# A two-layer transformer trunk: the opening stage in another order, with its sums on ScalarE and its first modulation in column groups

## What is computed

```
sh1, sc1, gt1, sh2, sc2, gt2 = silu(cond) @ w_mod + b_mod          # 1024 -> 6 x 1024
h = rms_norm(x, norm1_g) * (1 + sc1) + sh1
q, k, v, u = h @ w_in                                              # 1024 -> 1280
x = x + gt1 * (concat(attention(q, k, v), pool_mixer(u)) @ w_out)
h2 = rms_norm(x, norm2_g) * (1 + sc2) + sh2
x = x + gt2 * conv_ffn(h2)                                         # 1024 -> 2 x 2816 -> 1024
```

## Time and profile before

| | us |
|---|---|
| median of 3 runs | 1548.91 (1543.1 to 1551.49) |
| the profiled execution | 1550.63 |
| its span in the trace | 1548.7 |
| start of the first `w_first` transfer | 8.26 |
| start of the first projection (`linear_pair` of layer 0) | 61.51 |

### The profile page before, as it was taken

One profiled execution on the slowest core, in us unless ns is written; L12 is line 12 of the kernel. 1 busy time (PEld: TensorE's weight loads), 2 busy tenths in 40 slices (PEclk: granted clock), 3 DMA queues, 4 the chain that ended last, 5 costly groups with the idle time before them and its releaser, 6 DMA issues.

```text
span 1548.7 us, 25735 instructions
## 1 busy us (share of the span) xinstructions
PE 1465.7 (95%) x10321; PEld 1431.0 (92%) x10321; DVE 907.4 (59%) x1366; ACT 519.4 (34%) x744; POOL 409.4 (26%) x266
## 2 busy tenths in 40 slices
PE   6997789999999999999999978998999999999996
PEld 5997668989999999999999967898999999999996
DVE  0497895879683738695646577436944323444333
ACT  2424664252232113223223467425223211323221
POOL 1165100214342004243311530020433200333320
PEclk9999899999999999999999989998999999999998
DMA  8252021514343524343431200031422321222311
GB/s 318 86 164 85 29 68 38 170 50 155 122 132 120 152 72 146 109 151 111 138 94 49 72 28 2 15 97 47 157 68 81 94 70 56 81 68 81 94 57 69
DMA packets 191825, 147.02 MB, mean 95 GB/s; under 512 B 4337, under 2 KB 179065, under 8 KB 190713
## 3 DMA queue, kind: packets, MB, share of 16 engines
q1 hardware_dynamic: 191160, 145.51, 30.4%
q10 hardware_dynamic: 576, 0.26, 0.1%
HBM read 142.87 MB, written 2.88 MB: 94 GB/s over the span
## 4 chain that ended last, share of the span: by engine, by line
PE 87%; DVE 6%; ACT 2%; issue 2%; POOL 1%; DMA 1%; SPq 0%; DVEq 0%; ACTq 0%; POOLq 0%
PE pair L1076 69%; PE pair L1093 5%; PE pair L1341 3%; PE pair L1319 2%; PE pair L1159 2%; PE pair L1306 2%; PE pair L1192 2%; DVE mod_acc L805 1%; DVE small L969 1%; POOL tree L480 1%; DVE q_st L906 1%; ACT tree L692 1%; DVE w_lo L782 1%; PE pair L1146 1%; PE pair L1134 0%
## 5 line engine op out<-in xcount | busy, mean ns | idle before, releaser
L1076 PE MATMUL pair<-in_hi,w_hi 128*128 128x320 f32 x1792 | 411.7, 311 | 7.7 <-DVE w_lo L782 7.7
L1076 PE MATMUL pair<-in_hi,w_lo 128*128 128x320 f32 x1792 | 409.3, 310 | 0.0
L1076 PE MATMUL pair<-in_lo,w_hi 128*128 128x320 f32 x1792 | 408.8, 310 | 0.0
L1076 PEld LDWEIGHTS pair<-in_hi,w_hi 128*128 128x128 f32 x1792 | 300.2, 188 | 9.3 <-issue 6.3
L1024 DVE SCALAR_TENSOR_TENSOR conv<-pair,vec,conv 128x127 f32<-128x127 f32 x352 | 168.8, 541 | 236.3 <-ACT conv L720 236.1
L1076 PEld LDWEIGHTS pair<-in_lo,w_hi 128*128 128x128 f32 x1792 | 300.5, 188 | 0.0
L1076 PEld LDWEIGHTS pair<-in_hi,w_lo 128*128 128x128 f32 x1792 | 300.1, 188 | 0.0
L511 POOL TENSOR_TENSOR silu_a<-silu_a,conv 128x640 f32<-128x640 f32 x44 | 110.8, 2519 | 587.0 <-DVE conv L1024 587.0
L782 DVE TENSOR_TENSOR w_lo<-w_raw,w_hi 128x1024 fp32r<-128x1024 f32 (+1 forms) x152 | 203.8, 1342 | 82.9 <-ACT w_hi L532 82.7
L720 ACT ACTIVATE conv<-pair,vec 128x640 f32<-128x640 f32 x88 | 77.7, 885 | 438.1 <-PE pair L1076 427.4
L805 DVE SCALAR_TENSOR_TENSOR mod_acc<-mod_raw,cond,mod_acc 128x1024 f32<-128x1024 f32 x140 | 221.5, 1623 | 0.1
(11 more groups left out here) (146 smaller groups left out, 1600.9 us busy)
## 6 DMA issues: line engine op xcount, KB each, us to landing
w_raw<-in_w_up_dram SPq DMA_DIRECT2D x88, 512.0 KB, 3.9
mod_raw<-in_w_mod_dram SPq DMA_DIRECT2D x80, 512.0 KB, 4.1
w_raw<-in_w_down_dram SPq DMA_DIRECT2D x32, 704.0 KB, 4.7
w_raw<-in_w_in_dram SPq DMA_DIRECT2D x20, 512.0 KB, 4.2
w_first<-in_w_mod_dram SPq DMA_DIRECT2D x8, 1024.0 KB, 14.2
w_raw<-in_w_out_dram SPq DMA_DIRECT2D x16, 512.0 KB, 3.9
out_dram<-yout SPq DMA_DIRECT2D x5, 512.0 KB, 4.0
xin<-in_x_sample_dram SPq DMA_DIRECT2D x1, 2048.0 KB, 17.6
```

Source lines behind the costliest of these rows:

```text
L1076: ins = pe.matmul(dst[:, a:a + HALF_T], w[:, s, k, :], rhs[:, kk, a:a + HALF_T], start=first and r == 0, stop=last and r == 2)
```

## The change

x is loaded ahead of everything large, in five transfers with a semaphore each. The 14 row transfers go to ScalarE's queue, 5 ahead of its first activation and 9 behind its second. ScalarE squares each token block of `xin` as it lies (1024 columns, tokens on partitions), with a row sum as a by-product (`accum_out`), and takes the root of the five sums; GpSimd's adds and `stat(0)` go. The slices of x are copied out of PSUM by ScalarE (even k, bank `pair[2]`) and VectorE (odd k, bank `pair[3]`). After `spread(0)` VectorE makes `xhat` = x * rstd in the space of `xin`. The modulation swaps its operands: the stationary one is `cond_cols` (two conditioning columns and 30 of zeros), the moving one is `w_first`, 512 columns at a time, and its four quarters write to four groups of 32 partitions of one bank. Its result is copied out by ScalarE, transposed by four matmuls, and read by `mod_finish`. `in_hi` then is one ScalarE instruction from `xhat` with gain and shift, and VectorE makes its own copy of the sum (`sq`) and subtracts. The first load of `mod_raw` waits for the squares, whose scratch it is. Later norms are as before but for their semaphore counts.

```diff
+        cond_cols = mod_acc[:, 0, 0:NK * QUAD].rearrange("p (k r) -> p k r", k=NK)
+        first_rows = mod_acc[:, 1, 0:512]
...
+                xhat = xin[:, :, :].rearrange("p b d -> p (b d)").rearrange("p (k t) -> p k t", k=NK)
...
@@ sync
+            for b in range(NT):
+                src = x_prompt[0] if b == 0 else x_sample[0, (b - 1) * P:b * P, :]
+                sp.dma_start(xin[:, b, :], src).then_inc(s_x[b], 16)
+            for k in range(NK):
                 load_first(k)
+                if k >= NK - 2:
+                    load_in(0, k - (NK - 2))
+            for n in range(2, 4):
+                load_in(0, n)
             sp.dma_start(cst[:, P:n_const], consts[:, P:n_const]).then_inc(s_const, 16)
-            for k in range(4, NK):
-                load_first(k)
-            for n in range(4):
-                load_in(0, n)
+            sp.wait_ge(s_xsq, NT)
...
@@ scalar
+            act_e.activation(cond_cols[:, :, 0:2], pair[2][0:P, 0:2 * NK].rearrange("p (c k) -> p k c", c=2),
+                             ACT.Silu).then_inc(s_c32, 1)
...
+            for b in range(NT):
+                act_e.wait_ge(s_x[b], 16)
+                if b >= 2:
+                    act_e.wait_ge(s_xsq, b - 1)
+                act_e.activation(mod_raw[:, b % 2, :], xin[:, b, :],
+                                 ACT.Square, accum_out=rtok[:, b:b + 1]).then_inc(s_xsq, 1)
+            act_e.wait_ge(s_eps, 2)
+            act_e.wait_ge(s_xsq, NT)
+            act_e.activation(rtok[:, :], rtok[:, :], ACT.Sqrt, bias=eps[:, 0:1], scale=1.0 / D).then_inc(s_sd, 1)
+            for k in range(0, NK, 2):
+                act_e.wait_ge(s_xt, k + 1)
+                act_e.activation(x[:, k, :], pair[2][:, 0:T], ACT.Copy).then_inc(s_xe, 1)
...
+            hi(0, 0, NK)
+            act_e.wait_ge(s_mfirst, NK)
+            act_e.activation(first_rows, pair[0][:, 0:512], ACT.Copy).then_inc(s_frow, 1)
+            hi(1, 1, NK)
...
@@ vector
-            for n in range(2):
-                lo(n, n, NK)
+            for k in range(1, NK, 2):
+                dve.wait_ge(s_xt, k + 1)
+                dve.tensor_copy(x[:, k, :], pair[3][:, 0:T]).then_inc(s_xe_dve, 1)
...
+                dve.tensor_tensor(xhat[:, k, :], x[:, k, :], lin[3], ALU.mult).then_inc(s_xhat, 1)
             dve.wait_ge(s_vec, 1)
+            lo(0, 0, NK)
             for C in range(2):
                 mod_finish(C)
+            lo(1, 1, NK)
...
@@ tensor
                 pe.wait_ge(s_first[k], 16)
-                rhs = cond[:, :, k:k + 1].to_broadcast([P, 2, HALF])
-                for j in range(2 * NK):
-                    a = j % NK * P
-                    ins = pe.matmul(pair[j // NK][:, a:a + P].rearrange("p (i r) -> p i r", i=2),
-                                    w_first[:, k % N_FIRST, j * P:(j + 1) * P], rhs,
-                                    start=k == 0 and j % 4 == 0, stop=k == NK - 1, skip_group_check=True)
+                for j in range(4):
+                    ins = pe.matmul(pair[0][j * QUAD:(j + 1) * QUAD, 0:512], cond_cols[:, k, :],
+                                    w_first[:, k % N_FIRST, j * 512:(j + 1) * 512], start=k == 0, stop=k == NK - 1)
                 ins.then_inc(s_mfirst, 1)
...
+            pe.wait_ge(s_frow, 1)
+            for t in range(4):
+                ins = pe.transpose(pair[1][:, t * P:(t + 1) * P], first_rows[:, t * P:(t + 1) * P], ident)
+            ins.then_inc(s_ft, 1)
```

More of the change, by code:

```diff
@@ L23 @@
 HALF = P // 2
+QUAD = 32
 EPS = 1e-6
@@ L214, in v @@
             return vec[:, L, place[0], ds(place[1] + i, n)]
-        s_const, s_rows, s_x = sem("const_loaded"), sem("rows_loaded"), sem("x_loaded")
+        s_const, s_rows, s_x = sem("const_loaded"), sem("rows_loaded"), [sem(f"x_loaded{b}") for b in range(5)]
         s_crow = sem("cond_rows_loaded")
@@ L448, in sq_slot @@
                 return sq[:, m % 2, :]
-            clear_sum(0)
-            for m in range(NK - 1):
-                add_squares(0, m)
+            pool.memset(cond_cols, 0.0).then_inc(s_c32z, 1)
             for L in range(DEPTH):
@@ L578, in _ @@
                 ins.then_inc(s_vec, 1)
[L579 to L588 removed]
+            hi(0, 0, NK)
+            act_e.wait_ge(s_mfirst, NK)
+            act_e.activation(first_rows, pair[0][:, 0:512], ACT.Copy).then_inc(s_frow, 1)
+            hi(1, 1, NK)
+            act_e.wait_ge(s_gain, 1)
+            act_e.wait_ge(s_mod, 2)
+            for k in range(NK):
+                act_e.wait_ge(s_xhat, k + 1)
+                for ci, a, b in SEG:
+                    act_e.activation(in_hi[:, k, a:b], xhat[:, k, a:b], ACT.Identity,
+                                     scale=gain[:, 0, 0, ci, k:k + 1],
+                                     bias=mod[:, 0, 0, ci, k:k + 1]).then_inc(s_hhi, 1)
             for L in range(DEPTH):
[L590 removed]
+                if L > 0:
+                    norm(2 * L, L, 0)
                 hi_third(tile_in(L) + 2, NK, w_third_in)
@@ L814, in mod_finish @@
                 if C < 2:
[L815 removed]
+                    dve.wait_ge(s_ft, 1)
                 else:
@@ L1200, in _ @@
             pe.transpose(pair[2][:, 0:2 * NK], cond_rows[:, :], ident[0:2 * NK, 0:2 * NK]).then_inc(s_vec_t, 1)
+            pe.wait_ge(s_c32, 1)
             pe.wait_ge(s_cond, 1)
+            for k in range(NK):
+                if k >= 2:
+                    if k % 2 == 0:
+                        pe.wait_ge(s_xe, k // 2)
+                    else:
+                        pe.wait_ge(s_xe_dve, k // 2)
+                for b in range(NT):
+                    if k == 0:
+                        pe.wait_ge(s_x[b], 16)
+                    ins = pe.transpose(pair[2 + k % 2][:, b * P:(b + 1) * P], xin[:, b, k * P:(k + 1) * P], ident)
+                ins.then_inc(s_xt, 1)
+            mod_first(0)
             N_ROW_DMAS = 5 + 4 + 3 + DEPTH
@@ L1204, in _ @@
             for L in range(DEPTH):
-                if L > 0:
+                if L == 0:
+                    pe.wait_ge(s_xe, NK // 2)
+                else:
                     pe.wait_ge(s_vec, L)
```

129 lines of the change are left out of this document (68 added, 61 removed).

## The result

| | before | changed |
|---|---|---|
| median of the runs | 1546.19 us (1543.1 to 1551.49, 4 runs) | 1529.02 us (1524.98 to 1530.1, 4 runs) |
| profiled execution, its span | 1550.6, 1548.7 us | 1529.39, 1527.6 us |
| start of `linear_pair` | 61.51 us | 40.74 us |
| its length | 15.57 us | 16.77 us |
| from its end to the end of the span | 1471.6 us | 1470.1 us |

The ratio of the medians is 0.987 with a 95% interval of 0.9844 to 0.9895: faster by 1.1 to 1.6%. The forecast was 1528.0 us in a range of 1522 to 1539. In the profiled executions the span lost 21.1 us: 20.8 at the start of the first projection, less 1.2 that the projection itself grew, and 1.5 in all that follows.

The account below looks back on a forecast made before the run. TensorE was taken to bound the opening, with memory close behind. Terms up to VectorE's last chain put `linear_pair`'s start at 38.9 instead of 61.51 us: 22.6 off 1550.6 gives 1528.0 us, range 1522 to 1539.

Parts of the forecast that it names:

- x transposes end: TensorE's transposes of the x slices in the opening: end between 21.8 (fast) and 25.0 us (slow), taken as 23.3.
- a modulation step: Eight records of 512 columns on TensorE, all four column groups at once: 0.92 us against 3.99 for the old step.
- spreading ends: TensorE's spreading for the norm, after modulation steps 0 and 1 and the rows: 1.60 us long, ending at 28.8.
- slice 7 lands: Load of the last `w_first` slice, behind `w_in` tile 0: lands at 33.0 us, TensorE and memory arriving together.
- `xhat` ends: VectorE's eight `xhat` slices from 28.8 us, 0.82 each, end at 35.4 and lead its chain to the projection's start.
- rival (1): Modulation: only two records run at a time, a step takes 1.84 us, start 45.1, time 1534.2; chance 0.22.
- The plain shift: After the opening: its gain arrives unchanged at the end, 1487 us from projection start to span end, within 3 us.
- half clock: First projection: left at 15.57 us; half clock lasting twice as long would lose 1.9 us, put into the range only.
- (2): Modulation: the four groups run one after another, start 59.9 us, time 1549.0, no change; chance 0.08.
- (3): Modulation: groups run serially and TensorE stays at half clock for half the steps, start 76.5, time 1565.6; chance 0.05.
- (4): ScalarE's row issues cost twice SP's, squares start 6.3 us later, start about 45, time 1534; chance 0.05.
- (5): Stage up to 155 us: a free-running load gives the gain back later, up to all of it, 1550; chance 0.02.

Follow-up runs that it names:

- early_slices: Changed kernel with slice 6 of `w_first` in its own space and slice 7 loaded ahead of `w_in` tile 0; 1528.35 us, ratio 0.9871 to the kernel before.
- kept_busy: Changed kernel with extra matmuls that nothing reads in TensorE's waits around the last modulation step; 1526.31 us, ratio 0.9852 to the kernel before.
- two_groups: Changed kernel with two column groups in each of two banks and two copies by ScalarE; 1527.64 us, ratio 0.986 to the kernel before.
- one_group: Changed kernel with all four modulation quarters on one group of 32 partitions, in four banks, with four copies; 1544.53 us, ratio 0.9972 to the kernel before.
- rows_on_sync: Changed kernel with the parameter rows back on SP's queue, ahead of x; 1533.09 us, ratio 0.9907 to the kernel before.
- the first four experiments: Changed kernel with one column group (1544.53 us), two (1527.64) or the old modulation shape (1542.87); the kernel before with the column groups alone (1542.78).

## Why the prediction was right, and where its terms were off

| step of the sum | said | measured |
|---|---|---|
| root done | 16.2 | 15.5 |
| x transposes end | 23.3 | 21.9 |
| a modulation step | 0.92 | 0.86 |
| spreading ends | 28.8 | 26.5 |
| slice 7 lands | 33.0 | 34.85 |
| last step ends | 34.4 | 36.88 |
| `xhat` ends | 35.4 | 32.5 |
| projection starts | 38.9 | 40.74 |
| its length | 15.57 | 16.77 |
| from its start to the span's end | 1487 | 1486.9 (second execution 1482.9) |

**Right.** Four groups at once, the largest term: the two records of the earlier trace rows that start before either's second record were the evidence, and it carried over from two groups to four. The Trainium skill, "TensorE: Matmul & The Clock Gate", Part 3, gives 3.07x for four row groups; here four column groups do in 0.86 us what one does in 3.43, a factor of 4.0, more than the page has for four. The prediction took the same part's rule, that matmuls start and end strictly in program order, to speak for rival (1), and wrote that the trace does not agree. It read its own rows too coarsely. In stretches of 0.01 us at line 1341 of the kernel before, one record is at work first and two from the next stretch on:

```profile
187.70:187.71 0.01, 0.01 (x1) 0.01 (x2) 1.00 0.00 0
187.71:187.72 0.01, 0.01 (x2) 0.01 (x2) 1.00 0.00 0
```

At line 1257 now it is one in 26.40:26.41, two in 26.41:26.42, four in 26.42:26.43. So the trace agrees with the page's order of starts. What decides the time is that a group doesn't wait for another group's second record, which comes 0.43 us later.

**Right, but with too narrow a test.** The plain shift was right too: the earlier trace rows had no load behind the projection that runs ahead by itself, and over twelve executions with ends from 53.2 to 77.1 us the remainder behind the first projection stayed within 1466.3 to 1473.0. But the prediction called itself wrong if the length from the projection's start to the end of the span differed from 1487 by over 3 us. The first execution of the changed kernel had 1486.9, the second 1482.9, so that bound was narrower than two executions of one kernel lie apart.

**Some terms too large, which changed nothing.** ScalarE had issued the rows at 8.5 us (said 9.1), and the squares came at 1.04 us each (said 1.1). The Trainium skill, "ScalarE: Activation LUTs", What ACT_TABLE_LOAD costs, puts a drain of 1.38 us behind a table load; here the root starts 0.02 us after the load's 1.28 (13.90 + 1.28, then 15.20). The transposes of the last six slices took 5.8 us, from 16.14 to 21.91 (said 6.4); as the prediction had it they began slowly, 1.33 us for the first five as in the slow row, and the last ten took 1.52. (The column PEclk says 1.00 for 14 to 20 us all the same; in this early stretch the lengths of the records tell more.) So everything up to the spreading was 0.7 to 2.3 us early, and VectorE's eight slices from 28.8 on, which the sum took into the last chain, ended at 32.5, 2.9 us early (0.74 a slice instead of 0.82).

**One term too small, which took over: memory.** The prediction had TensorE and memory arrive together and went on from TensorE and VectorE. It costed slice 7 at 33.0. x landed at 11.4 (said 10.6), the slices 0 to 5 from 14.2 to 27.3, 2.63 us apiece (said 2.51, 13.1 to 25.7), and behind them slice 6, tile 0 and slice 7 moved at 372 and 355 GB/s. From the first issue of x (1.96, with the fixed 2.42) to the landing of slice 7 the 11 MB took 2.77 us each. That is near the upper value, 2.74, which the earlier trace rows gave for a long load among others. It isn't the engines' pace for these 11 MB alone: by 34.85 they had moved 12.4 million bytes, where 11 MB are 11.5. The other 0.9 are mostly the parameter rows and tile 1, which the sum had left out; at 417 GB/s they would take 2.1 us (estimate), about what slice 7 was late. So the last step ended 2.5 us later than costed, 1.85 for the slice and the rest for half clock, and behind it stand 3.9 us (copy, transposes, modulation end, `in_hi`) on the chain. early_slices shows what of this the order in SP's queue was worth: 1.9 us of landing, 1.4 us of start.

**One term taken at nothing: half clock.** The sum left the projection at 15.57, since TensorE had idled before it in both kernels. In the changed kernel it idles for 3.98 us ahead of the last step and again behind it, the clock stays at 0.50 from 36 to 46 us, and kept_busy prices that: 0.9 us in the last step, 0.5 in the transposes, 2.56 in the projection, of which 3.75 reach the end. Of the 2.56, 1.36 was paid before as well (14.21 against 15.57) and 1.2 is new. It lay within the 1.9 us that the prediction had set aside for this in its range.

The two errors made the opening 3.0 us longer (57.5 against 38.9 + 15.57 = 54.5); the remainder, 1.5 us shorter, took back half, and 1529.4 against 1528.0 is left. That the figure came so close is in part luck: the remainder alone differs by 3.8 us between two executions of the changed kernel, and 1528.0 was worked out from the profiled execution before, 1550.6, one of the slower ones. (Against the median the prediction had said 1526.3; the median is 1529.0.) The gain was forecast as 22.6 us. The profiled executions have 21.2, the medians 17.2 here and 19.1 beside the second execution.

**The rivals.** (1) was not what happened, and its price was wrong: 6.2 us for two records at a time. two_groups has it at 2.1 us of start and 0.9 of end. Its eight steps did outlast the slices, as the rival said, but the price was reckoned against a forecast in which four groups could use their whole lead, and they spend it waiting for slice 7. A chance of 0.22 went to a case that, had it come true, would not have been seen in the time. (2) was priced well (59.9, measured 58.2 in one_group, four copies included). The half clock of (3) appeared in the modulation, but for one step, not for half of them. In (4) the issues on ScalarE cost what SP's did; rows_on_sync shows that moving them is worth 4.4 us by itself. (5) did not happen.

**Open.** The remainder behind the projection differs by up to 6.7 us between kernels that have it in common, and by 3.8 between two executions of the changed one (1470.1 and 1466.3). It goes with the granted clock of the whole execution: of the 25 executions of the kernel before beside the first four experiments, the five with a mean granted clock of 0.982 or more have spans of 1541.2 to 1542.1 us, the eight with 0.976 or less 1549.1 to 1551.4; the two of the changed kernel had 0.974 and 0.979. What lowers it in one execution and not in the next no run shows.

## What to carry to other kernels

Before a step is made faster, write the landing time of each thing that it consumes beside its own: here going from one group to two brought all of the gain, and going to four only lengthened a wait, in which the clock fell and took back what was left. Two parts that each remove one of two bounds close together must be measured together: 7.4 and 7.3 us apart were 19.6 in one. And when the DMA engines are full, count every byte that is in the queues until the transfer lands, also what is issued behind it, or price it by the slowest comparable row of the trace.

## What the runs showed of the hardware

fp32 matmuls with 32 columns of weights, in four column groups, run four at a time: 0.43 us for four records of 512 columns, the same 0.43 that one record takes by itself in one_group. The moving operands of four groups, each of 512 fp32 columns on 128 partitions, did not slow each other. A wait of 4 us on TensorE from 30.9 to 34.9 was followed by the 1.2 GHz level until 46 us, 5 us into a stretch in which it worked without a gap (projection 16.77 us, and 14.21 where the wait was filled); in two_groups, where it had worked until 38.8 and then waited twice (1.29 and 2.08 us), the projection began at full clock, and a pair of its records took 0.73 instead of 0.45 us only from 43.8 to 47 us. Matmuls with no reader, in the waits, kept the clock at full speed (PEclk 1.00 from 31 to 60 us in kept_busy), and slice 7 landed no later (34.8).
